# Experts of at most 64 rows in one packed block: two products per weight chunk in place of three

## The reference

```python
logits = (xf @ w_router) + b_router
top_logit, top_idx = lax.top_k(logits, TOP_K)
top_w = jax.nn.softmax(top_logit, axis=-1)
...
def expert_block(args):
    toks, e = args
    xb = xf[toks]
    return (jax.nn.silu(xb @ w1[e]) * (xb @ w3[e])) @ w2[e]
```

## Time and profile before

| | us |
|---|---|
| median of 3 runs | 1914.64 |
| lowest, highest | 1905.44, 1916.42 |
| span of the profiled execution, first to last instruction | 1919.3 |
| TensorE busy, of the span | 1731.4 (90%) |
| VectorE busy | 1421.4 (74%) |
| ScalarE busy | 1042.3 (54%) |
| mean granted TensorE clock | 0.953 |

### The profile page before, as it was taken

One profiled execution on the slowest core, in us unless ns is written; L12 is line 12 of the kernel. 1 busy time (PEld: TensorE's weight loads), 2 busy tenths in 40 slices (PEclk: granted clock), 3 DMA queues, 4 the chain that ended last, 5 costly groups with the idle time before them and its releaser, 6 DMA issues.

```text
span 1919.3 us, 22270 instructions
## 1 busy us (share of the span) xinstructions
PE 1731.4 (90%) x7882; PEld 1390.2 (72%) x7883; DVE 1421.4 (74%) x1201; ACT 1042.3 (54%) x817; POOL 25.5 (1%) x31
## 2 busy tenths in 40 slices
PE   1899979996999949989979989999899899999995
PEld 0787758885877727868868868887687687787784
DVE  7776877757676776877868866656588688787787
ACT  1465434433555326757747745554577576675773
POOL 0100000000000000000000000000000000000000
PEclk9998989998999969999999999999999999999998
DMA  9874458754665436987978965666599699799892
GB/s 367 309 271 144 154 186 315 275 182 171 249 214 179 145 115 240 357 327 274 362 288 306 363 253 197 219 219 219 180 354 380 236 362 363 278 359 344 300 362 83
DMA packets 210686, 503.98 MB, mean 263 GB/s; under 512 B 9137, under 2 KB 13409, under 8 KB 210481
## 3 DMA queue, kind: packets, MB, share of 16 engines
q1 hardware_dynamic: 208770, 496.15, 72.3%
q0 software_dynamic: 1712, 5.43, 0.9%
HBM read 500.50 MB, written 1.05 MB: 261 GB/s over the span
## 4 chain that ended last, share of the span: by engine, by line
PE 79%; DVE 10%; issue 8%; ACT 2%; DMA 1%; DVEq 0%; ACTq 0%; SPq 0%
PE ps L1241 22%; PE ps L1243 22%; PE ps L1242 22%; DVE w_lo L772 2%; PE ps L1247 2%; PE ps L1248 2%; PE ps L1644 2%; PE ps L1530 2%; PE ps L1686 1%; DVE mod_acc L797 1%; ACT w_hi L457 1%; DVE stats L817 1%; PE ps L1365 1%; DVE gates L966 1%; PE ps L1366 1%
## 5 line engine op out<-in xcount | busy, mean ns | idle before, releaser
L772 DVE TENSOR_TENSOR w_lo<-w_raw,w_hi 128x2048 fp32r<-128x2048 f32 x423 | 966.4, 2291 | 381.7 <-ACT w_hi L457 381.1
L457 ACT CAST w_hi<-w_raw 128x2048 fp32r<-128x2048 f32 x423 | 806.5, 1910 | 352.0 <-PE ps L1243 282.7
L1241 PE MATMUL ps<-w_hi,actT_hi 128*128 128x512 f32 (+1 forms) x1536 | 613.8, 400 | 60.0 <-issue 40.2
L1243 PE MATMUL ps<-w_hi,actT_lo 128*128 128x512 f32 (+1 forms) x1536 | 600.0, 391 | 0.0
L1242 PE MATMUL ps<-w_lo,actT_hi 128*128 128x512 f32 (+1 forms) x1536 | 599.4, 390 | 0.0
L1241 PEld LDWEIGHTS ps<-w_hi,actT_hi 128*128 128x128 f32 x1536 | 294.3, 192 | 132.3 <-issue 60.9
L1243 PEld LDWEIGHTS ps<-w_hi,actT_lo 128*128 128x128 f32 x1536 | 293.3, 191 | 61.6
L1242 PEld LDWEIGHTS ps<-w_lo,actT_hi 128*128 128x128 f32 x1536 | 294.8, 192 | 57.5 <-issue 1.0
L1241 PE MATMUL ps<-w_hi,gT_hi 128*128 128x512 f32 x536 | 213.1, 398 | 16.3 <-DVE gT_lo L1058 14.1
L1243 PE MATMUL ps<-w_hi,gT_lo 128*128 128x512 f32 x536 | 213.6, 398 | 0.0
L1242 PE MATMUL ps<-w_lo,gT_hi 128*128 128x512 f32 x536 | 213.2, 398 | 0.0
(11 more groups left out here) (225 smaller groups left out, 1070.3 us busy)
## 6 DMA issues: line engine op xcount, KB each, us to landing
w_raw<-in_exp_w_dram SPq DMA_DIRECT2D x336, 1024.0 KB, 7.0
w_raw<-in_ffn_w_dram SPq DMA_DIRECT2D x33, 1024.0 KB, 5.2
w_raw<-in_w_mod_mix_dram SPq DMA_DIRECT2D x24, 1024.0 KB, 8.1
w_raw<-in_w_mod_ffn_dram SPq DMA_DIRECT2D x24, 1024.0 KB, 5.3
w_raw<-in_w_gate_dram SPq DMA_DIRECT2D x24, 1024.0 KB, 5.7
w_raw<-in_w_in_dram SPq DMA_DIRECT2D x14, 1024.0 KB, 7.3
w_raw<-in_w_out_dram SPq DMA_DIRECT2D x8, 1024.0 KB, 5.1
w_raw<-in_w_branch_c_dram SPq DMA_DIRECT2D x4, 1024.0 KB, 5.0
```

The source lines that it names most:

```text
L457: nc.scalar.copy(w_hi[:, j % SPLIT, :], w_raw[:, i % RING, :]).then_inc(split_hi, 1)
L772: TTn(w_lo[:, j % SPLIT, :], w_raw[:, i % RING, :], w_hi[:, j % SPLIT, :].bitcast(F32), ALU.subtract).then_inc(piece_used, 1)
L1241: MM(to, hi, w_h, start=first, stop=False)
L1243: return MM(to, lo, w_h, start=False, stop=last)
```

## The change

The packed block is no longer only a second block. `packed=True` becomes `fb`, the number of the packed block: 1 as before, or 0 for an expert with at most 64 rows, which has that block alone. All three engines test for `count > HALF_P`, a fourth body of the loop. In it every product is a `packed_product`, and the `fold` steps are made for block 0. A packed expert waits for `packed_ready` before its first product. Further, `second_block` at the end of each expert goes: the gather of a second block and its copies now stand at the start of the expert that has one. The core of the diff:

```diff
-                def panel_events(stretch, panels, split_base, panel0, blocks, folds=None):
+                def panel_events(stretch, panels, split_base, panel0, blocks, folds=None, fb=None):
+                    whole = [b for b in range(blocks) if b != fb]
...
                             if folds is not None:
-                                A(fold[:, 0, 0:w], ps[HALF_P:P, HW1 + 2, 0:w], ACT.Copy).then_inc(fold_copied, 1)
-                            for b in range(1 if folds is not None else blocks):
+                                A(fold[:, 0, 0:w], ps[HALF_P:P, HW1 + 2 * fb, 0:w], ACT.Copy).then_inc(fold_copied, 1)
+                            for b in whole:
                                 ins = A(silu[:, b, 0:w], ps[:, HW1 + 2 * b, 0:w], ACT.Silu)
                             if folds is not None:
                                 act.wait_ge(fold_added, folds + 2 * p + 1)
-                                ins = A(silu[0:HALF_P, 1, 0:w], fold[:, 0, 0:w], ACT.Silu)
+                                ins = A(silu[0:HALF_P, fb, 0:w], fold[:, 0, 0:w], ACT.Silu)
                             ins.then_inc(silu_ready, 1)
...
-                            TTn(fold[:, m, 0:w], fold[:, m, 0:w], ps[0:HALF_P, (HW1, HW3)[m] + 2, 0:w], ALU.add).then_inc(fold_added, 1)
+                            TTn(fold[:, m, 0:w], fold[:, m, 0:w], ps[0:HALF_P, (HW1, HW3)[m] + 2 * fb, 0:w], ALU.add).then_inc(fold_added, 1)
...
-                            ins = (packed_product if b and packed else product)(
+                            ins = (packed_product if b == fb else product)(
...
-                        def expert(blocks, packed=False):
-                            if packed:
-                                pe.wait_ge(packed_ready, e + 1)
-                            for b in range(blocks):
-                                pe.wait_ge(xg_hi_ready[b], e + 1)
-                                pe.wait_ge(xg_lo_ready[b], e + 1)
+                        def expert(blocks, fb=None):
+                            pe.wait_ge(xg_hi_ready[0], e + 1)
+                            pe.wait_ge(xg_lo_ready[0], e + 1)
+                            if blocks == 2:
+                                gather(1, e + 1)
+                                pe.wait_ge(xg_hi_ready[1], e + 1)
+                                pe.wait_ge(xg_lo_ready[1], e + 1)
+                            else:
+                                pe.sem_inc(gathered_hi[1], 1)
+                                pe.sem_inc(gathered_lo[1], 1)
+                            if fb is not None:
+                                pe.wait_ge(packed_ready, e + 1)
...
                                 scatter()
-                                second_block(e + 1, e + 2)
...
                         with pe.Else():
-                            expert(1)
+                            with pe.If(count > HALF_P):
+                                expert(1)
+                            with pe.Else():
+                                expert(1, fb=0)
```

More of the change, by code:

```diff
@@ L756, in _ @@
                             with act.Else():
-                                expert(2, packed=True)
+                                expert(2, fb=1)
                         with act.Else():
-                            expert(1)
+                            with act.If(count > HALF_P):
+                                expert(1)
+                            with act.Else():
+                                expert(1, fb=0)
                     for t in range(TT):
@@ L1219, in _ @@
                             with dve.Else():
-                                expert(2, packed=True)
+                                expert(2, fb=1)
                         with dve.Else():
-                            expert(1)
+                            with dve.If(count > HALF_P):
+                                expert(1)
+                            with dve.Else():
+                                expert(1, fb=0)
                     dve.wait_ge(added, 4 * EXPERTS + 4)
@@ L1520, in _, with swiglu @@
                 open_sublayer(layer * 2 + 1, 0, 4)
-                def swiglu(stretch, panels, piece_base, panel0, blocks, e=None, turn_places=None, packed=False):
+                def swiglu(stretch, panels, piece_base, panel0, blocks, e=None, turn_places=None, fb=None):
                     def turn(p):
@@ L1527, in turn @@
                         for b in range(blocks):
-                            n = HALF_P if b and packed else P
+                            n = HALF_P if b and b == fb else P
                             for c in range(panels[p] // P):
```

68 lines of the change are left out of this document (28 added, 40 removed).

## The result

The changed kernel takes 1996.42 us (median of 4 runs, 1995.76 to 2001.08) against 1914.67: 4.45% more, interval 4.16 to 4.74%, +81.8 us. The forecast was 1968, slower, with 1996 as its upper end.

A forecast was written before the change was run, and what follows sets the result against it. TensorE bounds the kernel, with VectorE 2.1 us per panel behind and pacing packed panels. Panels +45.5, between experts +3 and clock +5 give +53.5 us; 1914.6 + 53.5 = 1968, range 1936 to 1996.

The forecast's parts named there:

- Which engine sets a packed panel, and its size: Packed experts' panels: VectorE paces them at 18.3 us against 16.98, with a 2.49 us hole behind the A-side add.
- Five experts' products: Products of the five experts with at most 64 rows: +9.1 us each, +45.5 us in all (38 to 50).
- The clock, +5: TensorE's clock in packed experts: falls to half clock during holes are possible, +5 us in all (0 to 27).
- Rival 3: Packed experts: the clock stays low throughout, +26 us each, +130 in all, 2045 us; chance 0.08.
- Between experts, +3 (-15 to +15): Gaps between experts: removed test -6, wait for VectorE's copy +6, fourth expert's moved gather +3; together +3 us.
- (b): Packed expert's start: the first product must wait for VectorE's copy of the low half, +6 us in all (0 to 12).
- (a): Expert's end: removing the second-block test saves between nothing and 20 us; taken as -6, since a nested test is added.
- (c): Fourth expert's start: its second block's gather moves behind the loop's jump, at half clock, +3 us (0 to 6).
- the entries: Work between experts, -15 to +15 us; the range's high end was summed as 50 + 10 + 22, giving 1996.
- Rival 1: Packed panels: the fold chain's hole is hidden, VectorE's panel 15.8 us, -42 us, total 1870; chance 0.08.
- The loads: Weight loads in packed panels: stay hidden, costing nothing while a panel takes over 15.5 us (6.29 MB at 406 GB/s).

The follow-up runs named there:

- own-tile: Changed kernel, but a one-block expert's packed tile is written when its rows are gathered, into unused actT_hi columns; 1993.2 us, ratio 1.0399 to the kernel before.
- no-fold: Changed kernel without the fold steps: silu and the gate product read one half of the packed result, dropping the tokens' low part; 1896.6 us, ratio 0.9910.
- own-bank: Changed kernel with ScalarE rounding the next piece before silu, and the gated tile turned into an idle PSUM bank in packed one-block experts; 1939.7 us, ratio 1.0145.
- small-first: Changed kernel with the test for at most 64 rows made first and its packed body first in the program; 1980.0 us, ratio 1.0355.

## Why the prediction was wrong

- **Which engine sets a packed panel, and its size: right.** VectorE, 18.3 us said, 18.09 measured, with the 2.49 us hole where it was said to be. Leaving the fold out takes it away; moving one ScalarE instruction leaves 1.08 us of it, and the bank of its own 0.36.
- **Five experts' products: right in kind, large by a fifth.** +9.1 us each said, +7.4 measured (131.9 against 124.5), 37 for 45.5. The panels cost about what was said, +1.1 for +1.3, and the stretch behind the last gate product is 0.7 to 2.2 us shorter than unpacked.
- **The clock, +5: the falls came, and cost 3 us at most.** At half clock TensorE spent 107 us of the five packed experts' products, against 23 before, but the panels stay at 18.1 us through it. Only behind the last gate product, in two of the experts, do 1.5 us each go with it, and in the first of them that was so before too (13.3 us against 11.7 in the others). Rival 3, a clock that stays low, is out: the clock is low for 17 to 25 of an expert's 131 to 133 us, and the panel shown has clock 1.00 with 2 us holes in it.
- **Between experts, +3 (-15 to +15): this step failed.** It measured +39.1, and the gaps ahead of the five grew by 6.9 us each on average, over the 3 us that the prediction had named as a sign of being wrong. Within it, (b): for the wait for VectorE's copy I used the 4.89 us of the fourth expert's entry for all packed experts and added up +6. But that expert is the second body of the program, and there the body is the fourth, one long jump further, and the jump to the loop's start took longer too: 10.2 us on average (50.9 / 5). And TensorE has the same jumps itself, for which I had counted nothing more; in the own-tile kernel, where nothing waits for the copy, 26.5 of the 34.6 us are still there. (a): the test that goes, -6 said, shows nothing in the kernel without the packed body. (c): the fourth expert's gather, +3 said, measured +5.4 to +6.4.
- As measured, the terms make +74.9 us of span: +36.9 and +39.1, and -1 from the rest. The median moved by 81.8, since the profiled execution stood 4.6 us over the median before and 2.2 under it after; the prediction had carried its 4.7 over unchanged. The range's upper end, 1996, took the entries at +10; 1996.4 is close to it only because the panels and the clock cost less than the upper end gave them.
- **Rival 1, the hole hidden: its panel was near, its total wasn't.** With the order changed and the bank of its own, panels of 15.97 us; said 15.8. The total of 1870 is a slip, since -42 and +3 make 1876. The kernel took 1939.7: the products gave -26 for -42, and the time between experts +38 for +3.
- **The loads: right that they stay hidden at 18 us, and 15.5 us as their floor was half a microsecond low.** With the raw slots drained it is 15.97 us, at 394 GB/s, not the 406 of the best 5 us; for as long as pieces lay ready a panel took 14.5.

## What to carry to other kernels

Before taking work from the busiest engine, add up the next engine's time for the same unit and the loads' time: here they stood 2.1 and 1.0 us behind 16.98, so a third of TensorE's products was worth about 12% of a panel while loaded pieces lay ready and 6% after that. The small steps that the packing needs turned this into a loss in the panels, and the way into the new body cost as much again. A chain that passes between two engines, both with a queue in fixed order, left the one that waits idle for 2.49 us here; look for work to put between its steps, as rounding the next piece before silu. In this kernel a body of code for a special case cost its jumps at every entry, several microseconds each and one behind the other, and a wait placed at its start inherited them from the slower engine.

## What was not expected of the hardware

A jump to a far part of the program took TensorE 3.3 to 8.5 us by its branch records, while others took 0.1 to 0.5; on VectorE, in the changed kernel, it was 2.4 to 5.3 from a branch to the next record. In the kernel before the way from one one-block expert to the next took 9.7 us in some cases and 15.2 in others with the same code on it. Part of it stands in the branch records: the jump to the one-block body took 4.5 to 5.5 us on the way to the second, third and sixth expert and 0.2 to the seventh and eighth. What decides that isn't settled here. The long jumps have a rule in the Trainium skill, page Runtime: NRT & Kernel Launch, section Instruction fetch mechanics: instructions are fetched ahead in sequence only, and a taken branch whose target lies outside the pages already held waits for a fetch. The runs agree as far as they go: the small-first kernel, in which the packed body stands ahead of the others, has 9 long branches on TensorE for 17. That a fetch is what the time goes into, no run here shows. The page gives no time for it.

Loads of 1 MB pieces held 394 to 402 GB/s over whole panels of the no-fold and own-bank kernels, with the DMA share at 1.04.
